# Four gate and value units of layer one, and three of layer two, multiply the rows before they are normalised

## The reference

```python
def rmsnorm(x, g):
    y = xf * lax.rsqrt(jnp.mean(xf * xf, axis=-1, keepdims=True) + EPS)
    return y.astype(x.dtype) * g
...
    qa, ka, va, ub, cq, ckv, kpe, ud, gate_in = split_cols(h @ lw['w_in'])
...
    ud = ud[..., :CONV_WIDTH] * jax.nn.sigmoid(ud[..., CONV_WIDTH:])
...
    y = lax.conv_general_dilated(xx, conv_w[:, None, :], window_strides=(1,), ...
```

## Time and profile before

| what | before |
|---|---|
| median of 3 runs | 2332.49 us (2331.91 to 2333.06) |
| span of the profiled execution | 2334.1 us |
| PE busy | 2267.3 us, 97% |
| DVE busy | 1309.4 us, 56% |
| POOL busy | 976.5 us, 42% |
| ACT busy | 862.2 us, 37% |
| mean granted TensorE clock | 0.990 |

### The profile page before, as it was taken

One profiled execution on the slowest core, in us unless ns is written; L12 is line 12 of the kernel. 1 busy time (PEld: TensorE's weight loads), 2 busy tenths in 40 slices (PEclk: granted clock), 3 DMA queues, 4 the chain that ended last, 5 costly groups with the idle time before them and its releaser, 6 DMA issues.

```text
span 2334.1 us, 39824 instructions
## 1 busy us (share of the span) xinstructions
PE 2267.3 (97%) x15066; PEld 2183.7 (94%) x15066; DVE 1309.4 (56%) x2354; ACT 862.2 (37%) x1686; POOL 976.5 (42%) x988
## 2 busy tenths in 40 slices
PE   7999999999999899999999999999999989999997
PEld 7999998888999899999999999988889989999997
DVE  7996553334237835727589865433332387275374
ACT  4015233444213534625420152334441246255252
POOL 4544454232563342333455545533326623333231
PEclk9999999999999999999999999999999999999998
DMA  5251121111222222222234411211113312223121
GB/s 182 93 188 65 51 73 55 37 41 32 90 99 82 73 91 73 85 78 80 68 135 140 128 57 60 67 48 41 41 32 105 106 60 87 81 82 100 64 85 61
DMA packets 70564, 187.84 MB, mean 80 GB/s; under 512 B 19824, under 2 KB 22480, under 8 KB 69392
## 3 DMA queue, kind: packets, MB, share of 16 engines
q1 hardware_dynamic: 62608, 165.64, 21.9%
q10 hardware_dynamic: 7808, 20.16, 2.5%
HBM read 173.47 MB, written 14.14 MB: 80 GB/s over the span
## 4 chain that ended last, share of the span: by engine, by line
PE 91%; DVE 7%; ACT 1%; issue 1%; ACTq 0%; DMA 0%; SPq 0%; DVEq 0%
PE gemm L700 45%; PE gemm L1179 17%; PE gemm L1169 14%; PE side L1179 3%; PE side L1169 2%; PE side L1052 2%; PE side L1032 1%; PE side L815 1%; PE side L983 1%; PE side L1039 1%; DVE act_lo L2251 1%; PE side L903 1%; DVE prod L1996 1%; DVE prod L1833 1%; DVE x L1999 1%
## 5 line engine op out<-in xcount | busy, mean ns | idle before, releaser
L673 POOL TENSOR_TENSOR ring_lo<-w_raw,ring_hi 128x512 fp32r<-128x512 f32 x232 | 308.6, 1333 | 580.4 <-ACT ring_hi L1630 580.4
L654 POOL CAST w_hi<-w_raw 128x384 fp32r<-128x384 f32 x376 | 221.5, 589 | 717.9 <-PE gemm L700 681.9
L656 POOL TENSOR_TENSOR w_lo<-w_raw,w_hi 128x384 fp32r<-128x384 f32 x376 | 450.8, 1199 | 30.1
L700 PE MATMUL gemm<-h_hi,w_hi 128*128 128x320 f32 x1664 | 416.8, 332 | 6.3 <-DVE square L1825 4.2
L700 PE MATMUL gemm<-h_hi,w_lo 128*128 128x320 f32 x1664 | 379.8, 309 | 0.0
L700 PE MATMUL gemm<-h_lo,w_hi 128*128 128x320 f32 x1664 | 379.5, 309 | 0.0
L700 PEld LDWEIGHTS gemm<-h_hi,w_hi 128*128 128x128 f32 x1664 | 282.6, 189 | 36.9 <-issue 17.1
L1179 PE MATMUL gemm<-act_hi,ring_hi 128*128 128x320 f32 x960 | 300.1, 313 | 16.1 <-ACT gemm L1681 9.5
L1179 PE MATMUL gemm<-act_lo,ring_hi 128*128 128x320 f32 x960 | 299.4, 312 | 0.0
L1179 PE MATMUL gemm<-act_hi,ring_lo 128*128 128x320 f32 x960 | 299.4, 312 | 0.0
L700 PEld LDWEIGHTS gemm<-h_lo,w_hi 128*128 128x128 f32 x1664 | 278.7, 188 | 0.0
(11 more groups left out here) (318 smaller groups left out, 4321.9 us busy)
## 6 DMA issues: line engine op xcount, KB each, us to landing
w_raw<-in_ws_ff SPq DMA_DIRECT2D x120, 512.0 KB, 3.2
w_raw<-in_ws_gate SPq DMA_DIRECT2D x64, 512.0 KB, 3.3
w_raw<-in_ws_in SPq DMA_DIRECT2D x44, 512.0 KB, 3.3
w_raw<-in_ws_proj SPq DMA_DIRECT2D x64, 256.0 KB, 2.6
w_raw<-in_ws_out SPq DMA_DIRECT2D x16, 512.0 KB, 3.2
w_raw<-in_ws_fd SPq DMA_DIRECT2D x16, 384.0 KB, 3.0
x_park<-x ACTq DMA_DIRECT2D x2, 2560.0 KB, 12.4
x<-x_park ACTq DMA_DIRECT2D x4, 1280.0 KB, 6.2
```

The source lines that it names most:

```text
L654: eng.tensor_copy(w_hi[s][:, cols], w_raw[s][:, cols]).then_inc(w_high.sem, 1)
L656: eng.tensor_tensor(w_lo[s][:, cols], w_raw[s][:, cols], w_hi[s][:, cols].bitcast(F32), ALU.subtract).then_inc(w_split.sem, 1)
L673: eng.tensor_tensor(lo, src, hi.bitcast(F32), ALU.subtract).then_inc(lo_plain.sem, 1)
L700: mm = eng.matmul(dst[:, hf, 0:HALF], w, r[k][:, cols] if r in (xu_hi, xu_lo) else r[:, k, cols], start=first and k == 0 and part == 0, st ...
```

## The change

RAW_UNITS = (4, 3): in layer one units 0 to 3, in layer two units 0 to 2 multiply the raw rows. In layer one ACT first makes all eight high parts and then the eight squares, into eight buffers of their own (`first_sq`), and DVE likewise all low parts, then the seven additions; the small matmuls between the tiles of unit 0 (`busy`) go; the sum of squares is multiplied before unit 2 and the spread in front of its sixth tile. ACT copies raw gate 0 out of the accumulator (`raw_gate`), DVE multiplies it by rstd. Gate 1 and, in layer one, value 1 leave through `first_out` into the space of `cq`. SP issues the weights of unit 1 ahead of the last two pieces of x. Units that take normalised rows are no longer interleaved.

```diff
+RAW_UNITS = (4, 3)
...
             for k in range(KT):
+                if k == KT - 2:
+                    eng.dma_start(w_raw[1][:, :], layer_of(io["ws_in"], 1)).then_inc(w_loaded[1].sem, 16)
                 eng.dma_start(x[:, k, :], io["x"][:, k, :]).then_inc(x_loaded[k], 16)
-            eng.dma_start(w_raw[1][:, :], layer_of(io["ws_in"], 1)).then_inc(w_loaded[1].sem, 16)
...
-                for u in range(2):
-                    psum(u, 0)
+                for u in range(RAW_UNITS[l]):
+                    psum(u % 2, u // 2)
                     for k in range(KT):
                         if u == 0:
-                            if l == 0 and k:
-                                busy(2, 6)
                             eng.wait_ge(xu_ready.sem, xu_ready.at(l, k + 1))
...
-                        elif l == 0 and k == 1:
+                        elif l == 0 and u == 2 and k == 0:
+                            layer_norm_sum(l, 0)
+                        elif l == 0 and u == 2 and k == 5:
                             spread_factor(l, 0)
-                        product(l, u, G[u], u, k, KT, xu_hi, xu_lo)
-                    if u == 0 and l == 0:
-                        layer_norm_sum(l, 0)
-
-                for k in range(KT + 1):
...
+                        product(l, u, G[u % 2], u % 2, k, KT, xu_hi, xu_lo)
+
+                for u in range(RAW_UNITS[l], 6):
+                    psum(u % 2, u // 2)
+                    products(l, u, G[u % 2], u % 2, KT, h_hi, h_lo, ready=h_tile(0) if u == RAW_UNITS[l] else None)
+                with eng.Fori(3, A_UNITS // 2) as i:
...
                 x_high(0, k)
-                square_x(0, -1, k)
+            for k in range(KT):
+                eng.activation(first_sq[k][:, :], x[:, k, :], ACT.Square).then_inc(sq_ready.sem, 1)
             sqrt_table()
+            eng.wait_ge(unit_done.sem, unit_done.at(0, 1))
+            for hf, cols in halves:
+                eng.activation(raw_gate[:, cols], G[0][:, hf, 0:HALF], ACT.Copy).then_inc(g_free[0].sem, 1)
...
-                for i in range(1, 4):
+                read_unit(eng, l, 2)
+                eng.activation(gate1, gate1, ACT.Sigmoid).then_inc(gate1_done.sem, 1)
+                for i in range(2, 4):
...
                     if k:
                         h_low(l, k - 1)
-                    if k == 3:
+                    if l == 0:
+                        if k == 0:
+                            read_unit(eng, l, 0)
+                            eng.tensor_tensor(sg[:, :], raw_gate[:, :], rstd[:, :], ALU.mult).then_inc(gate0_scaled, 1)
+                        elif k == 1:
+                            first_out(1, value0)
+                        elif k == 3:
+                            first_out(2, gate1)
+                        elif k == 6:
+                            first_out(3, value1)
+                    elif k == 0:
+                        first_out(0, sg)
+                    elif k == 3:
                         first_out(1, value0)
                 h_low(l, KT - 1)
+                if l:
+                    first_out(2, gate1)
+                eng.wait_ge(unit_done.sem, unit_done.at(l, RAW_UNITS[l]))
...
+                    if i == 1:
+                        eng.wait_ge(gate1_done.sem, gate1_done.at(l, 1))
+                        if l == 0:
+                            read_unit(eng, l, 3)
+                            eng.tensor_tensor(cvp[:, 1, CH:CH + NP], gate1[:, 0:NP], value1[:, 0:NP], ALU.mult)
```

More of the change, by code:

```diff
@@ L307, in encoder @@
         oTs, _ = sb("o_latent_sample", [P, NH, NS], F32, cq_at)
+        first_sq = [sb(f"first_square{k}", [P, T], F32, KT * T * 4 + T * 4 * k)[0] for k in range(KT)]
+        raw_gate, _ = sb("raw_gate", [P, T], F32, (KT - 1) * T * 4)
+        gate1, value1 = cq[:, 0, :], cq[:, 1, :]
         pw0p, pw1p, pws, pld = sq0, sq1, t2b, [t2a, sg]
@@ L398, in encoder @@
         glu0 = signal("first_glu", 1)
+        gate0_scaled = sem("first_gate_scaled")
+        gate1_done = signal("second_gate", 1)
+        glu1 = sem("second_glu")
         hi_ready = signal("h_high", 3 * KT)
@@ L1817, in _ @@
                 x_low(0, k)
-                add_square(0, -1, k)
+            for k in range(1, KT):
+                eng.wait_ge(sq_ready.sem, sq_ready.at(0, k + 1 - KT))
+                if k > 1:
+                    eng.wait_ge(sq_added.sem, sq_added.at(0, k - KT))
+                eng.tensor_tensor(ssum[:, :], first_sq[0][:, :] if k == 1 else ssum[:, :], first_sq[k][:, :], ALU.add)\
+                   .then_inc(sq_added.sem, 1)
             for l in range(L):
@@ L1824, in first_out @@
                     for hf, cols in halves:
-                        eng.tensor_tensor(dst[:, cols], rstd[:, cols], G[u][:, hf, 0:HALF], ALU.mult)\
-                           .then_inc(g_free[u].sem, 1)
+                        eng.tensor_tensor(dst[:, cols], rstd[:, cols], G[u % 2][:, hf, 0:HALF], ALU.mult)\
+                           .then_inc(g_free[u % 2].sem, 1)
                 for k in range(KT):
@@ L1834, in _ @@
                        .then_inc(t_ready.sem, 1)
-                    if k == 0:
-                        first_out(0, sg)
                     if k:
                         h_low(l, k - 1)
-                    if k == 3:
+                    if l == 0:
+                        if k == 0:
+                            read_unit(eng, l, 0)
+                            eng.tensor_tensor(sg[:, :], raw_gate[:, :], rstd[:, :], ALU.mult).then_inc(gate0_scaled, 1)
[8 more added lines that the diff above has]
+                    elif k == 3:
                         first_out(1, value0)
                 h_low(l, KT - 1)
+                if l:
+                    first_out(2, gate1)
+                eng.wait_ge(unit_done.sem, unit_done.at(l, RAW_UNITS[l]))
                 eng.wait_ge(vec_loaded.sem, vec_loaded.at(l, 16))
@@ L1857, in glu @@
                         return
+                    if i == 1:
[3 more added lines that the diff above has]
+                            eng.tensor_tensor(cvp[:, 1, CH:CH + NP], gate1[:, 0:NP], value1[:, 0:NP], ALU.mult)
+                            eng.tensor_tensor(cvs[:, 1, :, CH:CH + NQ], heads(gate1[:, NP:T]), heads(value1[:, NP:T]),
+                                              ALU.mult).then_inc(glu1, 1)
+                            return
                     eng.wait_ge(unit_done.sem, unit_done.at(l, 2 * i + 2))
                     read_unit(eng, l, 2 * i)
-                    g = G[1]
-                    eng.tensor_tensor(cvp[:, i, CH:CH + HALF], sg[:, 0:HALF], g[:, 0, 0:HALF], ALU.mult)\
+                    g, gate = G[1], gate1 if i == 1 else sg
+                    eng.tensor_tensor(cvp[:, i, CH:CH + HALF], gate[:, 0:HALF], g[:, 0, 0:HALF], ALU.mult)\
                        .then_inc(g_free[1].sem, 1)
-                    eng.tensor_tensor(cvp[:, i, CH + HALF:CH + NP], sg[:, HALF:NP], g[:, 1, 0:PT1], ALU.mult)
-                    eng.tensor_tensor(cvs[:, i, :, CH:CH + NQ], heads(sg[:, NP:T]), heads(g[:, 1, PT1:HALF]), ALU.mult)\
+                    eng.tensor_tensor(cvp[:, i, CH + HALF:CH + NP], gate[:, HALF:NP], g[:, 1, 0:PT1], ALU.mult)
+                    eng.tensor_tensor(cvs[:, i, :, CH:CH + NQ], heads(gate[:, NP:T]), heads(g[:, 1, PT1:HALF]), ALU.mult)\
                        .then_inc(g_free[1].sem, 1)
@@ L1885, in conv @@
                             if not sample:
-                                if i:
+                                if i == 1 and l == 0:
+                                    eng.wait_ge(glu1, 1)
+                                elif i:
                                     read_unit(eng, l, 2 * i + 1)
```

19 lines of the change are left out of this document (5 added, 14 removed).

## The result

| what | before | changed |
|---|---|---|
| median, device time | 2334.11 us (2331.91 to 2336.34, 16 runs) | 2337.82 us (2336.66 to 2340.82, 16 runs) |
| ratio | | 1.0017, 95% interval 1.0010 to 1.0024 |
| span of the profiled execution | 2334.1 us | 2337.9 us |
| mean granted TensorE clock | 0.990 | 0.989 |

The change costs 3.7 us (95% interval 2.3 to 5.6), where the prediction had +1.4. That is within the 0.2% which the prediction called "same" (4.7 us), but 0.3 us above the upper end of its range, and 3.9 above its 2333.9. Of these 3.9 us only 2.3 belong to the change. The other 1.6 are the base: the prediction stood on the median of three runs of the kernel before, 2332.49, and sixteen runs have 2334.11. On that base its range would have ended at 2339.1.

The account below looks back on a forecast made before the run. PE was taken as the bound (91% of 2334.1 us), with DVE's glu(2) deciding when unit 7 starts. Layer one +3.4 and layer two -2.0 gave +1.4 us, so 2333.9 us; range 2330 to 2337.5.

Parts of the forecast that it names:

- The bound and the place: PE some 8 us early at unit 7 of layer one, then stalled there until DVE's glu(2) frees the accumulator.
- Layer one: Unit 7 starting 0.7 us later plus 2.7 us lost to the clock: +3.4 us, from +1.1 to +5.5.
- (a): Layer one, the factor: DVE starts normalising later than 31.60 us, by +1.7 us (+1.0 to +2.3).
- (b): Layer one, DVE's added work: 20 operations for 18 in the normalising loop, +1.6 us.
- (c): Layer one, DVE's contention with POOL's splits: 0.15 to 0.58 us per us of POOL, +0.8 us (+0.4 to +1.6).
- The clock falls already in unit 0: Rival: in layer one's unit 0, without fillers, a clock drop delays the factor, 1.7 to 2.7 us more; chance 0.18.
- (d): Layer one, glu(1) on DVE: its earlier 0.70 us wait for unit 3 mostly goes, -0.5 us (0 to -0.7).
- (e): Layer one, granted clock near 0.50 behind PE's idle time before unit 7: +2.7 us (1.7 to 2.9).
- Layer two: Unit 7 starts at 1221.8 instead of 1223.8 us, with no clock drop: -2.0 us (-1.1 to -2.3).
- The splits of POOL cost DVE the upper rate in both layers: Rival: +0.8 us more in layer one, +0.9 more in layer two, 2335.6 us; chance 0.08.

Follow-up runs that it names:

- the taps experiment: 12 instead of 30 tap instructions between glu(1) and glu(2), the rest behind glu(3): changed kernel 2328.04 us, kernel before 2333.64 us.
- layer2_only: Changed kernel with layer one put back as before, three raw units in layer two: 2333.99 us, ratio 0.9999 against the kernel before.
- layer1_only: Changed kernel with layer two put back as before, four raw units in layer one: 2337.73 us, ratio 1.0016 against the kernel before.
- gap_covered: Changed kernel with 34 unread small matmuls between units 6 and 7 of layer one: 2334.77 us, ratio 1.0005 against the kernel before.

## Why the prediction was off

**The base.** 1.6 of the 3.9 us have nothing to do with the change. The prediction added its +1.4 to 2332.49, a median of three runs that lay 1.6 us below that of sixteen. Three runs were too few for a forecast within a few us. The change itself was 2.3 us dearer than forecast: 3.7 for 1.4.

**The bound and the place: right.** PE reached unit 7 some 8 us early and DVE's glu(2) ended the wait (7.97 us, forecast about 8); the taps experiment shows it.

**Layer one: right in sum, +3.50 us against +3.4, but partly by luck.** Two of its terms were off, (a) too low by 1.1 us and (b) with (c) too high by some 0.5, and they cancelled in part. (a) DVE's first product came at 34.39, +2.8 us against +1.7 (at most +2.3). The eighth low part was ready at 18.49, so the case in which POOL's split slows DVE (18.4) came in full:

```profile
9.87 8.62 DVE L1811 SCALAR_TENSOR_TENSOR x_gained_lo<-x,gain_mix,x_gained_hi 128x640 fp32r<-128x640 f32 x8 [3.93 <-ACT x_gained_hi L1289]
```

Unit 1 ended at 26.7 (forecast 25.2 to 26.5), and PE stood 0.29 us before the small matmuls at 27.02; from there on the steps ran as forecast (1.25 us for the small matmuls, 4.4 for five tiles, 1.8 to DVE). The rival "The clock falls already in unit 0" has fallen. It is the kernel before that has such a dip, behind waits of 1.22 and 1.31 us between the tiles of unit 0, and the prediction did not see it. Before, then changed:

```profile
22.00:27.00 5.00, 4.14 (x21) 4.15 (x21) 3.37 (x5) 2.22 (x3) 2.58 (x3) 0.66 0.64 169
```

```profile
12.00:31.00 19.00, 18.39 (x124) 17.63 (x123) 15.77 (x17) 10.46 (x17) 12.95 (x10) 1.00 0.80 271
```

(b) and (c): the loop took 20.28 us for 18.43, +1.85 against +2.4. With the 1.6 of (b) contention added only about 0.3, although POOL's time in it rose from 6.96 to 12.06 us. (d) From the last h_lo to the end of glu(2) 23.1 us for 23.9, -0.7 against -0.5; glu(1) at 58.86 waited for nothing. Sum +3.9 against 2.9 of slack: unit 7 started at 77.92, 1.1 late (forecast 0.7). (e) From there to the read of unit 8 16.74 us against 14.36, +2.4 against +2.7. The forecast of (a) was too low in every run: DVE's first product came between 34.4 and 35.7 us in the seven kernels with this head (forecast 32.6 to 33.9), and the loop ended between 54.6 and 55.7, against 49.2 to 52.1 in the four with the old one.

**Layer two: this is the step that failed.** It makes 2.0 of the 2.3 us by the medians: forecast -2.0, layer2_only 0.0 (in its trace -0.2, in that of the changed kernel +1.2). The term that was wrong is what POOL's splits cost DVE. The prediction said "Two more parts of POOL (5.3 us) fall beside the normalising: at 0.15 to 0.37 a us (4.95/13.32, this layer's own) +0.8 to +2.0; I take +1.1", and so it had unit 7 at -2.0 us. Measured: POOL worked 18.81 instead of 13.32 us in the loop (+5.5, as forecast) and the loop grew from 19.35 to 22.56 us: **+3.2**, beyond the upper end too. Behind it the second instruction of glu(0), which has two operands in SBUF, took 0.81 us for 0.28 (+0.5). DVE's first product stood 9.87 us behind the start of the layer for 9.36 (+0.5); that part is not of layer two's own edit, since PE's idle time ahead of the small matmuls, 0.59 us in the changed kernel, was also 0.53 in layer1_only, whose layer two is the old one. It was 0.3 to 0.6 us in all kernels with the new head of layer one, and none to 0.2 us in those with the old one; why is not known. Sum +4.2 against 3.1 us of slack: +1.1 in place of -2.0. The gap before unit 7 was 1.39 us (forecast about 0.5), with no loss of clock behind it. The pair for gate 1 was hidden in the wait of glu(0), as forecast (1.15 us of it became 0.35).

The mechanism was named, also as the rival "The splits of POOL cost DVE the upper rate in both layers", but its size was read wrongly. I put the time of every loop's operations with two SBUF inputs (each to the start of the next) beside 0.83 us each, their length with POOL quiet, and POOL's busy time beside them:

| loop | operations | excess us | POOL beside them us | rate |
|---|---|---|---|---|
| layer one, before | 16 | 3.4 | 6.7 | 0.51 |
| layer one, changed | 17 | 3.7 | 10.5 | 0.35 |
| layer two, before | 16 | 4.3 | 11.8 | 0.36 |
| layer two, layer1_only | 16 | 4.9 | 11.9 | 0.41 |
| layer two, changed | 16 | 7.5 | 17.4 | 0.43 |
| layer two, layer2_only | 16 | 6.8 | 17.5 | 0.39 |

The rate is 0.35 to 0.51 and differs between loops with the same list (layer two before and in layer1_only), so it seems to hang on which operations meet; that is argued, not tested. The 0.15 of step (c) was the difference of the first and the third of these loops, at 0.51 and 0.36, taken for a price; and the 1.1 us of layer two leaned on it. At 0.41, the mean of the six, 5.6 us more of POOL make +2.3; the other 0.9 us is that the earlier trace rows caught a cheap loop of before and the changed kernel got a dear one. In layer one the same luck ran the other way: the rate there was 0.51 before and 0.35 in the changed kernel, which is why (c) came out low. The rows of layer two show what is hit: the product takes 2.08 us at 1186.61 and again at 1198.54, against 0.89 alone, but the pair at 1192.46, which reads an accumulator, keeps its 0.87 although POOL splits at that moment:

```profile
1191.94 2.03 POOL L665 TENSOR_TENSOR w_lo<-w_raw,w_hi 128x640 fp32r<-128x640 f32 x1
```

The Trainium skill, GPSIMD Engine Reference, section 1, names contention with DVE instructions that have two SBUF inputs. The trace agrees, also for the taps, which read an accumulator: one at 1214.05 takes 0.75 us beside a split that starts at 1214.06:

```profile
1214.05 0.75 DVE L1938 SCALAR_TENSOR_TENSOR side<-conv_prompt,vec,side 128x512 f32<-128x512 f32 x1
```

```profile
1214.06 1.58 POOL L665 TENSOR_TENSOR w_lo<-w_raw,w_hi 128x640 fp32r<-128x640 f32 x1
```

What stays open: that the loop of layer two was 0.7 us shorter in layer2_only and gap_covered than in the other kernels with three raw units (reciprocal to the end of normalising 26.55 us for 27.26) fits the scatter of the rate, but what sets the rate was not tested; nor was the delay of unit 1 in layer one. The trace points at POOL's split of unit 1, which began at 14.01 beside the low parts, but no run undid the order of the weights and x alone.

## What to carry to other kernels

Before taking waits away from the bounding engine, find the instruction of another engine at which it will meet its next one, and where that stands in its list: here PE gained 8 us and gave them all back at glu(2), with a clock penalty, until 18 tap instructions moved behind it; then the same change was worth 5.6 us. Gathering several short waits into one long one can cost more than it saves: the 7.97 us cost 2.4 more behind them, the short ones in layer two (0.60 to 1.40 us) nothing. A short wait is not safe for that, as the dip in unit 0 of the kernel before shows. Take the base from more than three runs when the effect is of a few us. And price contention from several stretches by what overlaps, operation by operation; the difference of two stretches is no price.

## What the hardware showed beyond what I expected

- A 128 x 640 operation of DVE with two SBUF inputs takes 0.81 to 0.89 us alone and 1.0 to 2.2 us beside POOL's split; pairs that read an accumulator stay at 0.87. POOL is slowed as well; its split of five tiles in the changed kernel's loop:

```profile
1185.98 2.03 POOL L665 TENSOR_TENSOR w_lo<-w_raw,w_hi 128x640 fp32r<-128x640 f32 x1
```

The same operation of the kernel before, with DVE at its taps:

```profile
1210.99 1.58 POOL L656 TENSOR_TENSOR w_lo<-w_raw,w_hi 128x640 fp32r<-128x640 f32 x1
```

- The granted clock was 0.50 behind 4.09 us of idle time as behind 7.97, although 4.40 us of small matmuls stood ahead of the former; with 0.31 us of idle time it was 1.00. So in this place small matmuls of 128 x 128 held the clock when they reached to within 0.31 us of the work, and not when they ended 4.09 us before it.
